# Attention products of a two-block transformer kernel brought to full 128-row tiles, with the loops after them reordered (one Trainium2 core)

## The reference, cut to what matters

```python
# token mixer: 16 meta tokens are put ahead of the 256 (272 keys, 256 queries used)
proj = h @ w_in                       # fox q,k,v (8 heads of 64), forget, swa q (8 heads), swa k,v (2 heads), two gates
log_f = log_sigmoid(fa + forget_bias)
o_fox = softmax(qa @ ka.T * scale + c_q - c_k, causal) @ va          # c = cumsum(log_f)
o_swa = softmax with sink (qb @ kb.T * scale + bias(distance), window 128) @ vb   # 4 query heads share a key head
y = sigmoid(ga) * (o_fox @ w_branch_fox) + sigmoid(gb) * (o_swa @ w_branch_swa)
h = h + y @ w_out
# odd layer
bg, cg, hx = split(xn @ w_in, 3); u = cg * hx; y = causal_conv3(u); h = h + (bg * y) @ w_out
```

## Time and profile before

| | |
|---|---|
| three runs | 2525.44, 2527.6, 2530.93 us; median 2527.6 us |
| the profiled execution | 2527.19 us |
| its span, first to last instruction | 2525.3 us |
| PE busy | 2476.3 us (98%) |
| DVE busy | 1899.8 us (75%) |
| ACT busy | 1251.5 us (50%) |
| POOL busy | 125.8 us (5%) |
| mean DMA rate | 185 GB/s |
| granted TensorE clock, mean | 0.999 of 2.4 GHz |

### The profile page before, as it was taken

One profiled execution on the slowest core, in us unless ns is written; L12 is line 12 of the kernel. 1 busy time (PEld: TensorE's weight loads), 2 busy tenths in 40 slices (PEclk: granted clock), 3 DMA queues, 4 the chain that ended last, 5 costly groups with the idle time before them and its releaser, 6 DMA issues.

```text
span 2525.3 us, 48394 instructions
## 1 busy us (share of the span) xinstructions
PE 2476.3 (98%) x17792; PEld 2274.6 (90%) x17792; DVE 1899.8 (75%) x3685; ACT 1251.5 (50%) x2081; POOL 125.8 (5%) x99
## 2 busy tenths in 40 slices
PE   9999999999999999999999999999999999999999
PEld 8998988999999889998989999999879999778999
DVE  6789997666666888889996666666887757767774
ACT  6754874444444334455864444444344445445443
POOL 0042000000000000061000000000000000000000
PEclk9999999999999999999999999999999999999999
DMA  7445676666655554545776666655545554534555
GB/s 241 143 152 176 195 204 234 212 205 214 208 196 187 189 185 167 168 159 182 202 242 209 210 207 214 208 185 189 189 153 175 173 178 149 114 124 139 179 180 163
DMA packets 192504, 467.22 MB, mean 185 GB/s; under 512 B 81746, under 2 KB 83794, under 8 KB 191456
## 3 DMA queue, kind: packets, MB, share of 16 engines
q1 hardware_dynamic: 118736, 419.99, 50.4%
q0 software_dynamic: 6992, 25.81, 3.7%
q10 hardware_dynamic: 66624, 19.40, 3.2%
HBM read 442.53 MB, written 22.61 MB: 184 GB/s over the span
## 4 chain that ended last, share of the span: by engine, by line
PE 48%; DVE 3%; DMA 1%; ACT 1%; issue 0%; DVEq 0%; ACTq 0%
PE acc L842 14%; PE work L522 9%; PE work L524 9%; PE work L523 9%; PE acc L522 1%; PE acc L523 1%; PE work L856 1%; PE acc L524 1%; DMA ring<-in_gate_in 1%; DVE ring_lo L516 1%; PE work L1071 1%; PE work L1043 0%; DVE arena L2130 0%; PE work L697 0%; PE work L696 0%
## 5 line engine op out<-in xcount | busy, mean ns | idle before, releaser
L516 DVE TENSOR_TENSOR ring_lo<-ring,ring_hi 128x1024 fp32r<-128x1024 f32 x758 | 920.3, 1217 | 440.4 <-ACT ring_hi L510 438.7
L510 ACT ACTIVATE ring_hi<-ring 128x1024 fp32r<-128x1024 f32 (+1 forms) x798 | 832.5, 1051 | 466.3 <-PE acc L842 370.1
L522 PE MATMUL work<-normed_hi,ring_hi 128*128 128x256 f32 (+1 forms) x2512 | 714.2, 284 | 20.4 <-DVE ring_lo L516 13.1
L523 PE MATMUL work<-normed_lo,ring_hi 128*128 128x256 f32 (+1 forms) x2512 | 708.6, 282 | 0.0
L524 PE MATMUL work<-normed_hi,ring_lo 128*128 128x256 f32 (+1 forms) x2512 | 706.5, 281 | 0.0
L842 PE MATMUL acc<-ring_hi,weighed 128*128 128x512 f32 x2048 | 587.9, 396 | 4.8 <-DVE weighed L1951 4.8
L522 PEld LDWEIGHTS work<-normed_hi,ring_hi 128*128 128x128 f32 x2512 | 472.8, 188 | 34.6 <-DVE ring_lo L516 13.7
L523 PEld LDWEIGHTS work<-normed_lo,ring_hi 128*128 128x128 f32 x2512 | 473.7, 189 | 7.9
L524 PEld LDWEIGHTS work<-normed_hi,ring_lo 128*128 128x128 f32 x2512 | 472.1, 188 | 0.0
L842 PEld LDWEIGHTS acc<-ring_hi,weighed 128*128 128x128 f32 x2048 | 373.7, 188 | 83.9 <-DVE weighed L1951 5.2
L522 PE MATMUL work<-arena_parts,ring_hi 128*128 128x256 f32 (+1 forms) x1184 | 337.0, 285 | 3.4 <-DVE arena L2170 1.6
(11 more groups left out here) (289 smaller groups left out, 2499.7 us busy)
## 6 DMA issues: line engine op xcount, KB each, us to landing
ring<-in_u SPq DMA_DIRECT2D x256, 512.0 KB, 3.3
ring<-in_v SPq DMA_DIRECT2D x256, 512.0 KB, 3.3
ring<-in_ffn_in SPq DMA_DIRECT2D x88, 512.0 KB, 3.3
ring<-in_query SPq DMA_DIRECT2D x32, 512.0 KB, 3.3
ficients_of_later_chunks<-gate_b ACTq DMA_DIRECT2D x32, 512.0 KB, 4.6
arena<-ficients_of_later_chunks POOLq DMA_DIRECT2D x32, 512.0 KB, 4.1
ring<-in_ffn_out SPq DMA_DIRECT2D x32, 512.0 KB, 3.8
ring<-in_even_in SPq DMA_DIRECT2D x27, 512.0 KB, 4.3
```

The costliest lines, as they stand in the source:

```text
L510: act.activation(ring_hi[:, n % RING, 0:width], ring[:, n % RING, 0:width], ACT.Copy).then_inc(hi_ready, 1)
L516: eng.tensor_tensor(ring_lo[:, n % RING, 0:width], ring[:, n % RING, 0:width], ring_hi[:, n % RING, 0:width].bitcast(F32), ALU.subtract).t ...
L522: pe.matmul(out, w_hi, hi, start=start, stop=False, **more)
L523: pe.matmul(out, w_hi, lo, start=False, stop=False, **more)
```

## The change

- **Swa scores.** Each swa query half is rounded to fp32r by ACT and its low part made by DVE, the two stacked as 128 rows in `swa_q` (high rows of one half, low rows of the other). The two key heads get a high and a low copy in `swa_k`, each already on both halves of the rows. A score is then two fp32r products over 128 rows in place of one float32 product over 64. The ten splits (`swa_part`) are put beside units 3 to 12 on ACT and 5 to 14 on DVE.
- **Forget terms.** `forget_two` becomes one block of 128 rows: the high part in rows 0 to 7, the low part in rows 32 to 39, zeros elsewhere; `neg_head` has its -1 in both places and is loaded as 128 rows. The two products over 8 rows become one over 128.
- **Mix.** The values of a pair of heads (for swa: one key head written twice, which makes four ACT copies in place of two) are the 128 columns of one weight tile, so the product has 128 output rows, of which the reader uses one half; the last block runs over 128 rows, those past key 16 being zeros.
- **Turn.** The last transposes are full 128x128; the probabilities' buffer has 384 columns, its pad cleared once by POOL. For t = 1 ACT copies all three blocks in one instruction.
- **POOL** gets two more memsets before its table loads, and the pad memsets (with their waits) ahead of the wait for the bias table.
- **Branch.** The rounding of the sum moves from DVE to ACT (`branch` on ACT), and DVE makes the low part of slot c-1 between the gating and the sum of slot c.
- **Mix output.** `mix_out` runs k = 0..4 of c = 0 and of c = 1, then k = 5..7 of both, then the rest.
- **Odd.** For the first channel block, DVE splits a ring slot one step sooner: ahead of the `value` chain, and one more after L2038.

```diff
@@ PE, attend, score
-                        q = qk2[half, (0 if fox else 8) + h // 2, t * P:(t + 1) * P]
-                        kk = qk2[half, 4 + h // 2 if fox else 12 + h // 4, 0:keys]
-                        mm = pe.matmul(work[:, w % 4, 0:keys], q, kk, start=True, stop=not fox)
                         if fox:
-                            for x in range(2):
-                                mm = pe.matmul(work[:, w % 4, 0:keys], neg_parts[0:FOXH, h, :], forget_two[0:FOXH, x, 0:keys], start=False, stop=(x == 1))
+                            q = qk2[half, h // 2, t * P:(t + 1) * P]
+                            pe.matmul(work[:, w % 4, 0:keys], q, qk2[half, 4 + h // 2, 0:keys], start=True, stop=False)
+                            mm = pe.matmul(work[:, w % 4, 0:keys], neg_parts[:, h, :], forget_two[:, 0:keys], start=False, stop=True)
+                        else:
+                            for x in range(2):
+                                mm = pe.matmul(work[:, w % 4, 0:keys], swa_q[:, h, t * P:(t + 1) * P], swa_k[:, h // 4, x, 0:keys], start=(x == 0), stop=(x == 1))
@@ turn
                         for b in range(t + 2):
-                            lo, hi = b * P, min((b + 1) * P, keys)
-                            mm = pe.transpose(work[0:hi - lo, w % 4, b * P:(b + 1) * P], scores2[:, u % 4, lo:hi], ident)
+                            mm = pe.transpose(work[:, w % 4, b * P:(b + 1) * P], scores2[:, u % 4, b * P:(b + 1) * P], ident)
@@ mix
-                            rows, t = min(P, TA - b * P), max(b - 1, 0)
-                            v = val2[0:rows, h // 2, b, (h % 2) * HD2:(h % 2 + 1) * HD2] if fox else \
-                                val2[0:rows, 4, b, (h // 4) * HD2:(h // 4 + 1) * HD2]
-                            mm = pe.matmul(work[half, w % 4, t * P:S], v, prob2[0:rows, u % 2, b, t:NT, :].rearrange("p t q -> p (t q)"),
+                            t = max(b - 1, 0)
+                            v = val2[:, h // 2 if fox else 4 + h // 4, b, :]
+                            mm = pe.matmul(work[:, w % 4, t * P:S], v, prob2[:, u % 2, b, t:NT, :].rearrange("p t q -> p (t q)"),
                                            start=(b == 0), stop=(b == NT), skip_group_check=True)
@@ PE, mix output (was: linear("mixout", ...))
+            def mix_out():
+                n, w0, soon = SLOT0["mixout"], W0["mixout"], K - 3
+                order = [(c, k) for ks in (range(soon), range(soon, K)) for c in range(2) for k in ks] + [(c, k) for c in range(2, K) for k in range(K)]
+                for c, k in order:
...
+                    mm = product3(pe, work[:, w % 4, 0:S], n + c, k, normed_hi[:, k, XS], normed_lo[:, k, XS], k == 0, k == K - 1)
@@ ACT, beside the units
+                    if 3 <= u < 3 + SWA_PARTS:
+                        whole, high, _ = swa_part(u - 3)
...
+                        act.activation(high, whole, ACT.Copy).then_inc(swa_hi, 1)
@@ ACT, branch (was: split_all("branch"))
+            def branch():
+                split_to(SLOT0["branch"])
+                for c in range(K):
+                    split_to(SLOT0["branch"] + c + 1)
+                    act.wait_ge(branch_sum, c + 1)
+                    act.activation(normed_hi[:, c, XS], mix_y[:, c % 2, :], ACT.Copy).then_inc(branch_hi, 1)
@@ DVE, odd
-                    split_to(SLOT0["odd"] + i)
+                    split_to(SLOT0["odd"] + i + int((kind, c) == ("value", 0)))
...
+                        if c == 0:
+                            split_to(SLOT0["odd"] + i + 2)
@@ DVE, beside the units
+                    if 5 <= u < 5 + SWA_PARTS:
+                        whole, high, low = swa_part(u - 5)
+                        dve.wait_ge(swa_hi, u - 4)
+                        dve.tensor_tensor(low, whole, high.bitcast(F32), ALU.subtract).then_inc(swa_lo, 1)
@@ DVE, branch
+                    if c:
+                        low_part(c - 1)
                     for x in range(2):
                         dve.wait_ge(*freed(w + x))
-                    dve.tensor_tensor(mix_y[:, b, :], mix_t[:, b, 0, :], mix_t[:, b, 1, :], ALU.add).then_inc(vec.sem, vec.up())
-                    step()
-                    parts(c, XS, mix_y[:, b, :], branch_ready)
+                    if c >= 2:
+                        dve.wait_ge(branch_ready, c - 1)
+                    dve.tensor_tensor(mix_y[:, b, :], mix_t[:, b, 0, :], mix_t[:, b, 1, :], ALU.add).then_inc(branch_sum, 1)
+                low_part(K - 1)
```

More of the change, by code:

```diff
@@ L55 @@
 NB = 32
+HALF_ROW = 32
 EVEN_ITEMS = [
@@ L399, in build @@
         qk2raw = view("mix", [BEHIND, TA])
-        scores2_at = used["mix"]
+        parts_at = used["mix"]
         qk2sq = view("mix", [BEHIND, TA])
-        scores2 = arena[:, scores2_at:scores2_at + 4 * (TA + 4)].rearrange("p (b t) -> p b t", b=4)
+        swa_q = weighed.rearrange("p e x t -> p (e x) t")
+        swa_k = arena_parts[:, parts_at:parts_at + 4 * TA].rearrange("p (g x t) -> p g x t", g=2, x=2)
         qk2ms = view("mix", [BEHIND, TA])
         bias2 = view("mix", [NT, FOXH, TA])
-        val2 = view("mix", [5, 3, P])
+        val2 = view("mix", [6, 3, P])
         prob2 = view("mix", [2, 3, 2, P])
@@ L421, in build @@
         w_forget = view("mix", [K, FOXH])
+        forget_two = view("mix", [TA], arena_parts)
         mix_y = view("after", [2, S])
@@ L477, in freed, with swa_part @@
             return bank_free[w % 4], w // 4 + 1
+        def swa_part(i):
+            if i < 2:
+                return qk2[:, 12 + i, :], swa_k[:, i, 0, :], swa_k[:, i, 1, :]
+            h = i - 2
+            own_half, other_half = [slice(x * HD2, (x + 1) * HD2) for x in (h % 2, 1 - h % 2)]
+            return qk2[own_half, 8 + h // 2, 0:S], swa_q[own_half, h, :], swa_q[other_half, h, :]
         def plain(n, k, cols):
@@ L617, in _ @@
             pool.wait_ge(stream_ready, 5)
+            pool.memset(val2[:, :, 2, :], 0.0).then_inc(memset_done, 1)
+            pool.memset(forget_two[:, :].bitcast(F32), 0.0).then_inc(memset_done, 1)
             pool.memset(table[:, :], NEG).then_inc(memset_done, 1)
@@ L632, in _ @@
                            table_out[0:FOXH, :].unsqueeze(1).to_broadcast([FOXH, P, DTAB])).then_inc(table_stored, 16)
+            pool.wait_ge(*freed(W0["mix"] + MIX_ITEMS.index(("turnf", 0))))
+            pool.wait_ge(forget_lo, 1)
+            for t in range(NT):
+                n = META + P * (t + 1)
+                pool.memset(scores2[:, t::NT, n:P * (t + 2)], 0.0).then_inc(pads_ready, 1)
             pool.wait_ge(table_stored, 16)
@@ L1460, in mix @@
                     if kind == "forget":
-                        act.activation(neg_parts[0:FOXH, :, :], neg_head[0:FOXH, :, :], ACT.Copy)
+                        act.activation(neg_parts[:, :, :], neg_head[:, :, :], ACT.Copy)
                         act.activation(small[:, 7:8], eps_col, ACT.Exp)
@@ L1491, in mix @@
                         act.wait_ge(*done(w))
-                        act.activation(val2[:, 4, 0:2, :], work[:, w % 4, 0:S].rearrange("p (t d) -> p t d", t=2), ACT.Copy)
-                        act.activation(val2[0:META, 4, 2, :], work[0:META, w % 4, S:S + P], ACT.Copy).then_inc(bank_free[w % 4], 1)
+                        for g in range(2):
+                            twice = lambda v: v.rearrange("p t (x d) -> p t x d", x=2)
+                            cols2 = slice(g * HD2, (g + 1) * HD2)
+                            main = work[:, w % 4, 0:S].rearrange("p (t d) -> p t d", t=2)[:, :, cols2]
+                            act.activation(twice(val2[:, 4 + g, 0:2, :]), main.unsqueeze(2).to_broadcast([P, 2, 2, HD2]), ACT.Copy)
+                            meta = work[0:META, w % 4, S + g * HD2:S + (g + 1) * HD2]
+                            ins = act.activation(val2[0:META, 4 + g, 2, :].rearrange("p (x d) -> p x d", x=2), meta.unsqueeze(1).to_broadcast([META, 2, HD2]), ACT.Copy)
+                        ins.then_inc(bank_free[w % 4], 1)
                     elif kind == "turnf":
                         act.wait_ge(forget_ready, 1)
-                        act.activation(forget_two[0:FOXH, 0, :], forget[0:FOXH, 0, :], ACT.Copy).then_inc(forget_hi, 1)
+                        act.activation(forget_two[0:FOXH, :], forget[0:FOXH, 0, :], ACT.Copy).then_inc(forget_hi, 1)
                         empty(w, forget_col, work[:, w % 4, 0:NT * FOXH].rearrange("p (t h) -> p t h", t=NT))
@@ L1551, in _ @@
             attend()
-            split_all("branch")
+            branch()
             split_and_square("mixout", 7, XS)
@@ L2217, in fixed_arrays @@
     late = {"foxmask": np.stack([np.where(cols[None, :] <= META + P * t + q, 0.0, NEG) for t in range(NT)], axis=1).astype(f)}
-    eye = np.eye(FOXH)
-    late["neg_head"] = np.repeat(-eye[:, :, None], P, axis=2).astype(f)
+    late["neg_head"] = np.zeros((P, FOXH, P), f)
+    for h in range(FOXH):
+        late["neg_head"][[h, HALF_ROW + h], h, :] = -1.0
     def bucket(d):
```

51 lines of the change are left out of this document (37 added, 14 removed).

## The result

The kernel before took 2528.49 us (median of 4 runs, 2525.44 to 2530.93), the changed kernel 2510.83 us (4 runs, 2509.41 to 2512.21): ratio 0.9931, 95% interval 0.9914 to 0.9948. The medians are 17.7 us apart. The forecast was 2508.7, range 2503 to 2513.5. Later, beside another nine runs of before (median 2529.17), the changed kernel took 2511.45, ratio 0.9933, 0.9919 to 0.9946.

What follows compares the result with a forecast made beforehand. PE was taken to bound attention from 2206.91 on, gate weight loads before. Savings of 1.2 (odd), 13.6 (attention) and 4.05 (branch, mix output) sum to 18.9: 2527.19 becomes 2508.3, as a median 2508.7; range 2503 to 2513.5.

Steps and rivals of the forecast that it cites:

- PE is the bound from 2207 on, stops come with the shape: Attention: PE is the chain from 2206.91; each tile shape change costs 0.176 us; swa heads fall from 6.37 to 4.93.
- Fox heads ahead of 2207 save nothing, since the gate loads hold PE: Attention up to 2206.91: PE waits for gate weight loads during the 56.7 us bias write, so these heads gain nothing.
- Swa term: Attention: eight swa heads save 1.44 us each, at 4.93 per head in place of 6.37.
- first rival: Attention: the ACT and DVE round sets swa's pace, 5.3 per head, 3 us more: 2511.7; chance 0.09.
- Fox term with the hand-over: Attention from 2206.91: 2.4 fox heads save 1.09 us each, less 0.8 for added low parts leaving the DMA regime.
- The rest of attention: End of attention: the last two mixes and copies save 0.3 us more.
- Branch and mix output: Six branch pairs save 1.65 us net, mix output's first two blocks 2.4; together 4.05; the stop ahead of branch stays.
- Odd: Odd layer: an earlier ring slot removes PE's 1.41 us stop, 0.2 comes back three items later; net 1.2.
- The type rival: Attention: stops stay at a change of type or operand, so only streams shrink: 2519.5; chance 0.05.
- The rival of the gate loads: Attention before 2206.91: gate loads do not hold PE, five more fox heads save 1.09 us each: 2503.3; chance 0.06.
- The slower one: Attention: full-width weight loads are no longer hidden, 0.188 us each, 19.6 over some 10.4 heads: 2528.3; chance 0.03.

Runs made afterwards that it cites:

- narrow_mix: The changed kernel with attention's mix products 64 columns of weights wide again, same streams and same 128 rows; 2511.53 us (one run), swa heads 5.24 apart, fox 6.49.
- float_scores: The changed kernel with swa's scores as one float32 product over 64 rows again; 2519.75 us (one run), swa heads 5.95 apart.
- two_steps: The changed kernel with the bias table written to DRAM once and spread to its 128 copies from there; 2501.91 us, ratio 0.9898 to the kernel before.
- changed_again: The changed kernel as it is, run five times again beside the kernel before: 2508.76 to 2512.60 us; the profiled execution is the 2508.76.

## Why the prediction came out right, and where it was off

- **PE is the bound from 2207 on, stops come with the shape.** Right. Forecast 4.93 per swa head, measured 4.95. The price of a change of shape was read as 0.176; narrow_mix gives 0.15 for a change of width, float_scores 0.19 for one of rows.
- **Fox heads ahead of 2207 save nothing, since the gate loads hold PE.** Right, shown by two_steps from the other side: take the write away, and they run at PE's 6.18.
- **Swa term.** Forecast 11.5, measured 10.74. The step that was mis-sized is the round of ACT and DVE: I worked out 4.93 from one round, called it level with PE's 4.91 and took no loss. It is 5.1 on average. That is the first rival's mechanism; it costs two stops, 0.63 us, not 3, because ACT and DVE start with a lead that lasts for the first four heads. The other 0.16 is 0.02 a head that PE itself takes longer.
- **Fox term with the hand-over.** Forecast 2.4 x 1.09 - 0.8 = 1.8, measured 1.50. The hand-over itself was 0.05 and 0.46, less than the 0.8; but only two full periods lie behind it, not 2.4, and PE's own is 0.08 longer than forecast. The rest of attention gave 0.27, forecast 0.3.
- **Branch and mix output.** Forecast 4.05, measured 4.34 and 4.10. Pairs 2.80 apart, no stop in mix output. The stop ahead of branch, which I left at its size, grew from 1.90 to 2.33 us from start to start, as PE's work behind the last transposes shrank by 0.5 us and ACT's last sigmoids, with the load of their table ahead of them (1.28 us), did not.
- **Odd.** Forecast 1.2, measured 1.63 and 1.64. I took the idle time shown for the stop, 1.41, as its price. The products around it start 1.68 apart in place of 0.12, so it cost 1.56: the idle time begins only at the modelled end of the product ahead. And nothing came back three items later.
- **What no term had.** The granted clock. Two falls on PE's path, which the profiled execution of before does not have, took 3.3 us. That is most of the distance from 2508.7 to the profiled execution's 2512.2. The median came 2.1 late; its executions have mean clocks of 0.997 and 0.998, so the falls are the likely reason there too, but only one of them has a trace.
- **What was luck.** The sum of the work, 18.5 against 18.9, is nearer than its terms: attention fell 1.1 short of 13.6, while odd and branch with mix output gave 0.7 more than forecast.
- **Rivals.** The type rival is excluded by narrow_mix, where the type stayed and the stops came back, and by the float32 mix that takes its streams alone; its time should read 2519.9, since the sum started from the profiled 2527.2 where the other rivals start from 2527.6. The rival of the gate loads is excluded by two_steps. The slower one asked for bare full-width loads: narrow_mix excludes it too, and L1105's six products in 1.08 us are streams alone. The Trainium skill, page "TensorE: Matmul & The Clock Gate", section "Part 3: Packing small matmuls", lets a load overlap only across row groups in its list of what overlaps, and names the background weight buffer as a second case in the paragraph ahead. For full tiles these runs disagree with the list (24 products 0.118 apart, each with new weights) and are in line with the paragraph; the measurement decides.

What stays open: why a fall of the clock follows one stop and not another. In the traces here each fall inside attention, branch and mix output comes in a stop of PE of 1.5 to 3.0 us or within 2 us behind one, but the stop of 2.33 at the start of branch had one behind it in the first profiled execution of the changed kernel and none in changed_again or two_steps. And the rounds of 4.91 and 5.30 us take turns for a reason that I did not find.

## What to carry to other kernels

Where PE is the bound, keep consecutive products in one tile shape, even at the price of padding: in this kernel zero rows cost nothing where the columns streamed are the same, and each change cost PE 0.15 us or more. Where loads hold PE, as up to 2207 here, it gains nothing. Price a stop by the distance of the starts around it, not by the idle time shown. When PE gets faster, read the round trip through the other engines over several periods before calling it level, and look for long DMAs: one 57 us write was worth some 8 us, nearly half as much as this whole change.

## What the runs showed of the hardware that I had not expected

- 128 copies of 20.5 KB, read out of 8 partitions of SBUF, took 57 us (packets of 5248 bytes, 7 under way at a time) and made 512 KB loads beside them slow (7.8 us median); the same bytes spread from DRAM to DRAM took 11.9 us (packets of 20992 bytes, 12.6 under way), with loads at 3.3.
- The clock went to 1.2 GHz for some three microseconds (twice for some seven) in or behind some stops of PE of 1.5 to 3.0 us, on some executions of the same program and not on others: 1.5 to 1.8 us each where PE is the bound, next to nothing where PE waits. Much of the spread of a kernel's runs (2525.3 to 2530.3) goes with the mean clock (0.999 to 0.997).
- A full-tile float32 or fp32r product shows nothing of its weight load behind one of the same shape (fp32r 0.118 us apart, six float32 instructions of a mix in 1.08); a tile half as wide cost 0.15 us going in and 0.15 coming out.
